# Normalising attention probabilities: products with diagonal matrices replaced by an in-place scaling on GpSimd and plain transposes

## The reference

```python
for i in range(S // Q_BLOCK):                     # two blocks of 128 queries
    q0, q1 = i * Q_BLOCK, (i + 1) * Q_BLOCK
    s = einsum('bqhd,bkhd->bhqk', q[:, q0:q1], k[:, :q1]) * scale
    s = s + fcum[:, :, q0:q1, None] - fcum[:, :, None, :q1]
    s = where(causal, s, -inf)
    p = softmax(s, axis=-1)
    outs.append(einsum('bhqk,bkhd->bqhd', p, v[:, :q1]))
```

## Time and profile before

| | us |
|---|---|
| median of 3 runs | 1334.92 |
| lowest and highest run | 1333.04, 1335.80 |
| span of the profiled execution, first to last instruction | 1328.7 |
| the median less that span (the profiled execution's own time is not listed apart) | 6.2 |

### The profile page before, as it was taken

The page is one execution under the profiler, slowest core; times in us unless marked ns, Lnnn a source line. Parts: engine busy times, 40 slices in busy tenths (PEclk is TensorE's granted clock), DMA queues, the critical chain, the costliest instruction groups (busy, mean ns, idle before and its releaser), DMA issues.

```text
span 1328.7 us, 31283 instructions
## 1 busy us (share of the span) xinstructions
PE 1117.3 (84%) x13118; PEld 636.4 (48%) x13118; DVE 428.9 (32%) x1380; ACT 174.2 (13%) x420; POOL 21.1 (2%) x61
## 2 busy tenths in 40 slices
PE   5999989668998679767899989597799997797676
PEld 1885346224554235323474874363356663353233
DVE  0697252112332113212344440631133232132124
ACT  1114030001110001000100430400010110010011
POOL 1300000000000000000000000000000000000000
PEclk8899989779999779877999999798799998798788
DMA  9985599999999999999998631989999999999992
GB/s 356 382 330 221 223 422 419 421 420 421 421 420 420 420 421 420 420 421 419 420 415 327 287 127 64 380 366 420 420 421 420 383 404 420 421 421 420 421 420 121
DMA packets 77794, 494.77 MB, mean 372 GB/s; under 512 B 7876, under 2 KB 16100, under 8 KB 20856
## 3 DMA queue, kind: packets, MB, share of 16 engines
q1 hardware_dynamic: 76752, 490.77, 90.0%
q10 hardware_dynamic: 744, 2.35, 0.5%
q0 software_dynamic: 192, 0.15, 0.0%
HBM read 492.19 MB, written 1.05 MB: 371 GB/s over the span
## 4 chain that ended last, share of the span: by engine, by line
PE 54%; DMA 34%; SPq 4%; DVE 4%; ACT 2%; issue 1%; DVEq 0%; POOL 0%; POOLq 0%
PE PS L1126 23%; DMA ring<-in_w_up_dram 16%; DMA ring<-in_w_gate_dram 10%; PE PS L1023 6%; PE PS L1285 4%; SPq L460 4%; PE PS L921 3%; PE PS L1154 3%; PE PS L1104 2%; DMA work<-in_w_up_dram 2%; PE PS L1412 2%; PE PS L1041 2%; DMA work<-in_w_gate_dram 2%; DMA work<-in_w_down_dram 2%; DMA ring<-in_w_ada_dram 2%
## 5 line engine op out<-in xcount | busy, mean ns | idle before, releaser
L1126 PE MATMUL PS<-ring,work 128*32 128x256 f32 x8160 | 534.7, 412 | 130.0 <-DMA ring<-in_w_up_dram 52.3
L1126 PEld LDWEIGHTS PS<-ring,work 128*32 128x32 f32 x8160 | 272.0, 116 | 376.9 <-DMA ring<-in_w_up_dram 90.0
L1745 DVE TENSOR_TENSOR work<-work,PS 128x256 f32<-128x256 f32 x43 | 18.1, 421 | 399.0 <-PE PS L1126 399.0
L1023 PE MATMUL PS<-ring,work 128*128 128x512 f32 x192 | 83.4, 594 | 0.5 <-ACT work L853 0.5
L1126 PE MATMUL PS<-work 128*32 128x256 f32 x864 | 60.6, 417 | 13.4 <-DMA work<-in_w_down_dram 6.9
L1104 PE MATMUL PS<-hs,work 128*32 128x256 f32 x784 | 61.4, 436 | 11.7 <-DVE work L1693 11.7
L700 ACT ACTIVATE work<-PS 128x256 f32<-128x256 f32 x43 | 16.5, 384 | 408.1 <-PE PS L1126 408.1
L921 PE MATMUL PS<-ring,cact 128*32 128x512 f32 x384 | 51.1, 664 | 14.7 <-DMA ring<-in_w_ada_dram 14.7
L1154 PE MATMUL PS<-work 32*128 32x256 f32 x784 | 56.1, 400 | 3.8 <-DVE work L1758 3.8
L1285 PE MATMUL PS<-work,ring 128*128 128x256 f32 x256 | 58.1, 390 | 1.4 <-ACT work L632 1.4
L696 ACT ACTIVATE work<-PS 128x256 f32<-128x256 f32 x49 | 18.8, 384 | 303.5 <-PE PS L1104 303.5
(11 more groups left out here) (262 smaller groups left out, 873.1 us busy)
## 6 DMA issues: line engine op xcount, KB each, us to landing
ring<-in_w_gate_dram SPq DMA_DIRECT2D x116, 1024.0 KB, 26.6
ring<-in_w_up_dram SPq DMA_DIRECT2D x116, 1024.0 KB, 26.7
ring<-in_w_down_dram SPq DMA_DIRECT2D x116, 1024.0 KB, 26.2
ring<-in_w_ada_dram SPq DMA_DIRECT2D x48, 1024.0 KB, 18.3
ring<-in_w_pw_dram SPq DMA_DIRECT2D x12, 1024.0 KB, 18.4
work<-in_w_up_dram SPq DMA_DIRECT2D x12, 1024.0 KB, 20.1
work<-in_w_gate_dram SPq DMA_DIRECT2D x12, 1024.0 KB, 26.4
work<-in_w_down_dram SPq DMA_DIRECT2D x12, 1024.0 KB, 27.7
```

What stands on the lines that cost most here:

```text
L1023: last = pe.matmul(PS[:, banks + 2 * t + q, :], moving[:, k, t * P:(t + 1) * P], quarter(index + h, kk, KH)[:, q * BANK:(q + 1) * BANK], s ...
L1126: last = pe.matmul(dst[SLOTS * s:SLOTS * (s + 1), :], rows[:, cc, SLOTS * q:SLOTS * (q + 1)], quarter(load + h, kk, KH)[:, QUART * s:QUART ...
```

## The change

The four diagonals on DVE go away. DVE counts up a new semaphore, `rinv_ready`, after the reciprocal. POOL waits for it and multiplies the probabilities of the pair in PR in place by 1/(row sum), with four instructions (128 x 128 and 128 x 256, for each of the two heads), and counts up `p_ready`. PE then turns the six tiles by plain transposes with the identity. `weigh` takes both tiles of keys 0 in one matmul of 256 columns, so that a head has two matmuls (256 and 128 columns) and not three of 128.

```diff
+        rinv_ready = sem("rinv_ready")
...
             affine(OF_Q, FFN_G, FFN_B, (4, 1), (4, 0))
+            for i in range(PAIRS):
+                pool.wait_ge(rinv_ready, i + 1)
+                for r in range(2):
+                    for t in range(TT):
+                        of_tile = PR[:, i % 2, r, (0, P)[t]:(P, 3 * P)[t]]
+                        last = pool.tensor_scalar(of_tile, of_tile, rinv[:, i, 2 * r + t:2 * r + t + 1], None, ALU.mult)
+                last.then_inc(p_ready, 1)
             pool.wait_ge(col_copied, 5)
...
-                        last = pe.matmul(PS[:, 2 + r, n * P:(n + 1) * P], PR[:, i % 2, r, n * P:(n + 1) * P],
-                                         diagonal(i, 2 * r + (0, 1, 1)[n]), start=True, stop=True, skip_group_check=True)
+                        last = pe.transpose(PS[:, 2 + r, n * P:(n + 1) * P], PR[:, i % 2, r, n * P:(n + 1) * P], ident[:, :])
...
-                for n in range(3):
-                    t, k = (0, 1, 1)[n], (0, 0, 1)[n]
+                for k in range(TT):
                     for r in range(2):
                         h = 2 * i + r
-                        last = pe.matmul(PS[HD * r:HD * r + HD, i % 2, t * P:(t + 1) * P], V[:, k, h * HD:(h + 1) * HD],
-                                         PRT[r][:, n * P:(n + 1) * P], start=(n != 2), stop=(n != 1),
+                        last = pe.matmul(PS[HD * r:HD * r + HD, i % 2, k * P:SEQ], V[:, k, h * HD:(h + 1) * HD],
+                                         PRT[r][:, 2 * k * P:(2 + k) * P], start=(k == 0), stop=True,
                                          tile_position=(0, HD * r), skip_group_check=True)
...
-            def diagonals(i):
+            def shares(i):
                 dve.wait_ge(exp_done, i + 1)
-                link(dve.reciprocal(rinv[:, i, :], rsum[:, i, :]))
-                for n in range(4):
-                    last = dve.tensor_scalar(diagonal(i, n), ident[:, :], rinv[:, i, n:n + 1], None, ALU.mult)
-                last.then_inc(p_ready, 1)
+                dve.reciprocal(rinv[:, i, :], rsum[:, i, :]).then_inc(rinv_ready, 1)
```

More of the change, by code:

```diff
@@ L249, in trunk_kernel @@
         assert at[0] <= 7168 - SEQ
-        def diagonal(i, s):
-            return (QT, KT)[s // 2][:, i, (s % 2) * P:(s % 2 + 1) * P]
         PS = ctx.enter_context(nc.psum_tensor("PS", [P, 8, BANK], F32))
@@ L1957, in _ @@
                 if i >= 1:
-                    diagonals(i - 1)
+                    shares(i - 1)
                     copy_pT(i - 1)
```

## The result

| | before | changed |
|---|---|---|
| median, us | 1334.13 (4 runs) | 1344.17 (4 runs) |
| lowest and highest run | 1333.04, 1335.80 | 1343.40, 1348.36 |
| span of the profiled execution | 1328.7 | 1341.8 |
| from the start of the first scores to the output product | 58.9 | 67.8 |

The medians are 10 us apart (0.8%); the ratio of changed to before, worked out from the runs, is 1.0091 [1.0073, 1.0109], so the change costs 0.7% to 1.1%. The forecast was 1333.9 us with a range up to 1340.0. The result lies outside it, in the direction of rival 2.

A forecast was written before the change was run, and what follows sets the result against it. PE was taken to bound the attention, with transfers following it. Turning -4.02, pair 0 +0.26, tail +1.02 and clock +1.70 gave -1.04 us on a span of 1328.7; with 6.2 carried to the median, 1333.9 us, range 1329.5 to 1340.0.

The forecast's parts named there:

- rival 2: Attention: POOL's chain takes 2.63 us, over the 1.95 us of cover, so PE waits at every pair; 1340.5 us, chance 0.22.
- What bounds the kernel: PE limits the attention, transfers limit the experts; time won or lost in the attention moves the end by the same amount.
- Turning, -0.67 a pair: Six transposes on PE cost 0.67 us in place of 1.34; over six pairs behind a query, -4.02 us.
- Weighing and DVE at nothing: Wide weigh on PE taken as 0 (-0.4 to +0.1 us over eight pairs); dropping covered diagonals, pairs 0 to 5, gives nothing.
- POOL's price: Four scalings a pair on POOL cost 1.46 us like AFFINE_SELECT (0.99 to 2.53), 1.56 with two hand-overs.
- The page's rule: One-input operations on POOL run roughly at line rate: 768 columns an estimated 0.64 us and overheads.
- Cover, 1.95 us: Time from a pair's reciprocal to PE being free to turn: 1.95 us at five pairs, 1.30 at pair 0 (+0.26 us).
- Tail, +1.02: Last scores to output product: 14.02 us in place of 13.00, with gaps of 3.23 and 2.29 and PE's clock low.
- Clock, +1.70 behind: Output product: PE's clock stays low for its first 3.4 us, which costs 1.70 us.
- Carry-over of 6.2 us: The runs' median lies 6.2 us above the profiled span of 1328.7; this difference was added to the forecast span.
- Rival 5: Transposes let PE's clock fall while queries run: about +40 us over six pairs, 1375 us; chance 0.02.

The follow-up runs named there:

- one head each: The changed kernel with one head of each pair scaled by DVE and the other by POOL; 1334.78 us, ratio 1.0022 to the kernel before.

## Why the prediction was wrong

The place of the loss was foreseen, as a rival; the step that failed is POOL's price, a term of the sum that was taken at half of what it is. The terms in order:

- **What bounds the kernel.** Right. PE set the pace of the attention, and what was lost there went through SP's waits (51.0 to 54.0 and 52.1 to 57.4 us) to the end.
- **Turning, -0.67 a pair.** Right where the turn follows PE's own work: 0.66 with the scaling on DVE and with the reciprocal early. Behind a wait it takes 0.87, and 0.47 are saved. (The old turn too takes 1.60 behind a gap at full clock and 1.34 without; why is not shown.) The sum had no such case, and rival 2, which has a wait at every pair, should have counted 0.47 and not 0.67: 1.2 us over six pairs.
- **Weighing and DVE at nothing.** Right: 0.80 against 0.81 us, and attention 67.9 against 67.8 with the old weigh. That a diagonal less on DVE gives nothing while queries run is right too.
- **POOL's price. This step failed.** I took 1.46 us by AFFINE_SELECT, between 0.99 and 2.53. It was 2.99, above the upper bound, and the two hand-overs 0.15, not 0.10. "A scaling too reads one tile, does one operation and writes one" was the reason, and it is no reason: on this engine a copy, a select and a multiplication of the same tile have different prices (0.38, 0.46 and 0.91 us for 256 columns). The upper bound was none either. I had held two inputs for the dearest case; a scaling, with one tile, costs more than TENSOR_TENSOR's 0.76 us.
- **The page's rule.** I cited the Trainium skill, "GPSIMD Engine Reference", section "Engine selection", for one-input operations at roughly line rate, an estimated 0.64 us. The measured 2.99 us is over four times that; here the measurement decides. It did not enter the sum.
- **Cover, 1.95 us.** Right to 0.01: 3.14 - 1.18 = 1.96. Pair 0: 3.14 - 1.30 = 1.84, as measured. With the price right, my own sum gives 5 x 1.19 + 1.84 = 7.8 us of waits.
- **Tail, +1.02.** It was +3.95. Of the difference of 2.93, the two gaps are +3.14 (each 1.57 longer than 3.23 and 2.29), the turns and weighs at the low clock +0.36 against my halves, and the last weigh -0.55, as the clock had returned (to 0.02).
- **Clock, +1.70 behind.** Not seen in the first profile: the output product began at the upper level. It was seen in the second, and with one head each: 4.9 us at the low level, not 3.4, so +2.4 us and not +1.70. (In the trace of before the clock rose at 794.4 us, 3.5 us after the turn began at 790.85.) The forecast had this as its main case; the profiles show both outcomes.
- **Carry-over of 6.2 us.** Wrong in what it is. A run lies 1.7 to 1.8 us above its span in every later record. The rest was that the profiled execution of before was a quick one (about 1330.4 by its span, against 1334.1). The changed kernel's profiled execution, 1343.55, is near its median of 1344.17, so 6.2 does not hold for it, and 3 of the 13 us between the two spans are not between the medians.
- **Rivals.** Rival 2 is what happened, with its place right and its price too low. Its threshold, 1.85 us, fits: 1.65 us with one head each brought no wait, 2.99 did; no run lies nearer. I gave it 0.22, and the range stopped inside it, at 1340.0. With 2.99 in its terms, 0.47 saved a pair and the tail as measured it gives -2.82 + 7.8 + 3.95 = +8.9. On 1328.7 and 6.2 that would be 1343.8 us, close to the measured 1344.2, but by luck: the carry-over is too large for the changed kernel, and 4.2 us outside the attention, which no term had, stand in for it. Rival 5, clock lost to transposes while queries run, was not seen: with the scaling on DVE the granted clock is 1.00 from the first to the last scores (743.3 to 785 us), and a turn takes 0.66 us. There the rule that I cited for it has no effect on the time.

## What to carry to other kernels

A price that no row shows is not bounded by other operations of the same engine that look alike, as the one instruction decides: eleven instructions at the start of a program, where nothing waits, settle it in one run. Hold a step moved to another engine against its cover, from the moment its input is ready to the moment its reader is free. Where the price is above it, an earlier start can take the wait away as well as a faster engine can, as the early reciprocal did at five pairs. And read a stretch of a few us behind a gap from two profiles or more, since the clock may come back in one and not in the other.

## What the runs showed of the hardware

- POOL multiplies a float32 tile by a column in some 0.28 us plus 2.4 to 2.5 ns for each column (0.30, 0.58, 0.91 us for 8, 128 and 256), and copies 128 and 256 columns in 0.27 and 0.38. DVE takes 0.28 and 0.35 us in the attention for what takes POOL 0.60 and 0.92.
- POOL and DVE scaling tiles in SBUF side by side slow one another, 602 to 746 ns and 349 to 460 ns, each by less than an instruction of the other takes.
- A float32 transpose of 128 columns costs PE 0.11 us, half of a product of the same size. PE's clock stood at 1.00 in a stage with 5.97 us of products to 0.66 of transposes a pair.
- The same program had PE's clock back before the output product in one execution and 4.9 us behind its start in another. Keeping PE at work in two gaps of 4.8 and 3.9 us kept the clock at 1.00 and gave 2.7 us back.
